# The fourth head of a cross attention: values in halves and other PSUM banks

## The reference

```python
def cross_attend(xn, mk, mv, w_xq, w_xo):
    B, L = xn.shape[:2]
    q = (xn @ w_xq).reshape(B, L, N_X_HEADS, X_HEAD_DIM)
    s = jnp.einsum('bqhd,bkhd->bhqk', q, mk.astype(q.dtype)).astype(F32) * (X_HEAD_DIM ** -0.5)
    p = jax.nn.softmax(s, axis=-1).astype(q.dtype)
    o = jnp.einsum('bhqk,bkhd->bqhd', p, mv.astype(q.dtype))
    return o.reshape(B, L, X_WIDTH) @ w_xo
```

## Time and profile before

| what | us |
|---|---|
| runs, median | 1565.68 |
| profiled execution, whole | 1566.68 |
| profiled execution, its span | 1564.8 |
| TensorE busy in the span | 1517.6 |
| VectorE busy | 653.5 |
| ScalarE busy | 446.4 |
| GpSimd busy | 227.5 |
| mean granted clock of TensorE | 0.988 |

### The profile page before, as it was taken

How to read it: one execution, slowest core, us unless ns; L and a number is a source line. 1 busy time by engine, 2 the same in 40 slices (tenths; PEclk the granted TensorE clock), 3 DMA queues, 4 the chain that set the end, 5 groups by cost and what they waited for, 6 DMA issues and landing times.

```text
span 1564.8 us, 24482 instructions
## 1 busy us (share of the span) xinstructions
PE 1517.6 (97%) x9798; PEld 1446.6 (92%) x9798; DVE 653.5 (42%) x1230; ACT 446.4 (29%) x828; POOL 227.5 (15%) x231
## 2 busy tenths in 40 slices
PE   6999999999899899999999999999999999999997
PEld 6999888888799888878899999999999999999997
DVE  5544666464855433443274322233223432234222
ACT  6422444333421222432143310233102321133122
POOL 2100000133355100034350000000000000000143
PEclk9999999998899999999999999999999999999999
DMA  7554011111231200064531111111111111111102
GB/s 216 180 177 129 28 35 34 41 45 55 87 123 54 94 28 28 14 220 157 175 108 41 53 41 52 43 41 54 41 54 41 40 54 41 54 41 41 54 27 111
DMA packets 153553, 115.49 MB, mean 74 GB/s; under 512 B 13680, under 2 KB 142896, under 8 KB 153200
## 3 DMA queue, kind: packets, MB, share of 16 engines
q1 hardware_dynamic: 142736, 79.11, 17.2%
q0 software_dynamic: 8544, 31.04, 5.8%
q10 hardware_dynamic: 2192, 4.20, 0.8%
HBM read 101.19 MB, written 14.16 MB: 74 GB/s over the span
## 4 chain that ended last, share of the span: by engine, by line
PE 87%; DVE 4%; issue 3%; DMA 2%; ACT 2%; POOL 1%; SPq 0%; DVEq 0%; ACTq 0%; POOLq 0%
PE ps L334 25%; PE ps L335 25%; PE ps L336 25%; PE ps L1165 4%; PE ps L1571 2%; PE ps L1553 1%; DVE wlo L321 1%; PE ps L1253 1%; PE ps L1277 1%; ACT whi L316 1%; DVE rstd L1734 1%; DMA raw<-in_w_xv 1%; DMA raw<-in_w_in 1%; DMA raw<-in_w_xk 1%; PE ps L1632 0%
## 5 line engine op out<-in xcount | busy, mean ns | idle before, releaser
L334 PE MATMUL ps<-xhi,whi 128*128 128x352 f32 x1392 | 457.6, 329 | 5.9 <-DVEq L2250 2.2
L335 PE MATMUL ps<-xlo,whi 128*128 128x352 f32 x1392 | 449.0, 323 | 0.0
L336 PE MATMUL ps<-xhi,wlo 128*128 128x352 f32 x1392 | 448.9, 322 | 0.0
L334 PE MATMUL ps<-yhi,whi 128*128 128x352 f32 x1152 | 377.3, 327 | 5.9 <-DVE wlo L321 2.1
L336 PE MATMUL ps<-yhi,wlo 128*128 128x352 f32 x1152 | 370.3, 321 | 0.0
L335 PE MATMUL ps<-ylo,whi 128*128 128x352 f32 x1152 | 370.1, 321 | 0.0
L334 PEld LDWEIGHTS ps<-xhi,whi 128*128 128x128 f32 x1392 | 263.6, 189 | 15.3 <-issue 11.6
L335 PEld LDWEIGHTS ps<-xlo,whi 128*128 128x128 f32 x1392 | 264.0, 190 | 0.1
L336 PEld LDWEIGHTS ps<-xhi,wlo 128*128 128x128 f32 x1392 | 263.3, 189 | 0.0
L316 ACT ACTIVATE whi<-raw 128x1024 fp32r<-128x1024 f32 x130 | 137.1, 1055 | 387.0 <-PE ps L336 343.6
L334 PEld LDWEIGHTS ps<-yhi,whi 128*128 128x128 f32 x1152 | 216.7, 188 | 10.0 <-DVE wlo L321 3.9
(11 more groups left out here) (260 smaller groups left out, 1295.7 us busy)
## 6 DMA issues: line engine op xcount, KB each, us to landing
raw<-in_w_up SPq DMA_DIRECT2D x32, 512.0 KB
raw<-in_w_down SPq DMA_DIRECT2D x32, 512.0 KB
raw<-in_w_xo SPq DMA_DIRECT2D x16, 512.0 KB
kx<-in_cache_mem_k POOLq DMA_DIRECT2D x16, 512.0 KB, 5.2
raw<-in_w_in SPq DMA_DIRECT2D x14, 512.0 KB
spill<-hT POOLq DMA_DIRECT2D x8, 528.0 KB, 6.3
xin<-in_x_prompt SPq DMA_DIRECT2D x8, 512.0 KB, 7.7
raw<-in_w_xk SPq DMA_DIRECT2D x8, 512.0 KB
```

Source lines behind the costliest of these rows:

```text
L334: pe.matmul(out, whi[:, q, k, :], x1, start=k == 0, stop=False)
L335: pe.matmul(out, whi[:, q, k, :], x2, start=False, stop=False)
L336: mm = pe.matmul(out, wlo[:, q, k, :], x1, start=False, stop=k == KB - 1)
```

## The change

Three things move.

1. `cross_values` can do one half d of its work. Group 5's halves stand ahead of and behind the four score tiles 24 to 27; group 6's halves stand between transpositions. `s_xo` counts up only after the half d=1.
2. Tiles 28 to 31 are transposed into banks 0 and 1 (`turned_bank`), and group 7's values go to banks 4 and 5. The transpositions no longer wait for the copy of the group before.
3. On VectorE `cross_keep(5)` stands behind `cross_max(12)`, on ScalarE behind `cross_exp(12)`, and `cross_pT(7)` ahead of `cross_hi(6, 0)`. The wait for `s_xol` at XRES stands ahead of the transpositions of b=0, kb=1, where it stood ahead of the first `xo_product`.

```diff
         def cross_bank(j, d):
-            return (0 if j == 2 * XH - 1 else 6) + d
+            return (4 if j == 2 * XH - 1 else 6) + d
+
+        def turned_bank(j):
+            return 0 if j == 2 * XH - 1 else 4
...
             for k in range(4):
                 kept_hi(k)
+            cross_exp(12)
             cross_keep(5)
-            cross_exp(12)
             kept_hi(4)
...
             cross_exp(15)
+            cross_pT(7)
             cross_hi(6, 0)
-            cross_pT(7)
...
             def cross_turn(i):
                 pe.wait_ge(s_xp, i + 1)
-                wait(pe, s_xpe, i // 4)
+                if i // 4 < 2 * XH - 1:
+                    wait(pe, s_xpe, i // 4)
...
-            cross_values(5)
+            cross_values(5, (0,))
             pe.wait_ge(s_ev, chunks_before(U_XO))
             i = 3 * NQ
             for t in range(4):
                 cross_scores(i + t)
+            cross_values(5, (1,))
             turns_and_scores(i)
-            cross_values(6)
-            for t in range(4, NQ):
-                cross_turn(i + t)
+            cross_turn(i + 4)
+            cross_turn(i + 5)
+            cross_values(6, (0,))
+            cross_turn(i + 6)
+            cross_turn(i + 7)
+            cross_values(6, (1,))
             cross_values(7)
...
                     pe.wait_ge(s_kl[slot], b // 2 * 16 + 16)
+                    if b == 0 and kb == 1:
+                        pe.wait_ge(s_xol, XRES)
...
             kept_lo(0)
             kept_lo(1)
+            cross_max(12)
             cross_keep(5)
-            cross_max(12)
             kept_lo(2)
             cross_probs(12)
```

More of the change, by code:

```diff
@@ L1004, in cross_pT @@
                 wait(act, s_xo, j - 1)
-                copy(xpT[:, :, cross_half(j)], ps[:, 4:6, :]).then_inc(s_xpe, 1)
+                copy(xpT[:, :, cross_half(j)], ps[:, turned_bank(j):turned_bank(j) + 2, :]).then_inc(s_xpe, 1)
             def cross_keep(j):
@@ L1557, in cross_turn, with cross_values @@
                 pe.wait_ge(s_xp, i + 1)
-                wait(pe, s_xpe, i // 4)
+                if i // 4 < 2 * XH - 1:
+                    wait(pe, s_xpe, i // 4)
                 for a in range(2):
-                    mm = turn(ps[:, 4 + a, (i % 4) * P:(i % 4 + 1) * P], xp[:, i % NQ, a * P:(a + 1) * P])
+                    mm = turn(ps[:, turned_bank(i // 4) + a, (i % 4) * P:(i % 4 + 1) * P], xp[:, i % NQ, a * P:(a + 1) * P])
                 mm.then_inc(s_xpT, 1)
-            def cross_values(j):
+            def cross_values(j, parts=range(2)):
                 pe.wait_ge(s_xpe, j + 1)
@@ L1567, in cross_values @@
                     wait(pe, s_xol, 8 if j == 6 else j)
-                for d in range(2):
+                for d in parts:
                     k = j // 2 * 2 + d
@@ L1571, in cross_values @@
                         mm = pe.matmul(ps[:, cross_bank(j, d), :], mv[:, a, k * P:(k + 1) * P], xpT[:, a, cross_half(j)], start=a == 0, stop=a == 1)
-                mm.then_inc(s_xo, 1)
+                if d == 1:
+                    mm.then_inc(s_xo, 1)
             def turns_and_scores(i):
@@ L1654, in _ @@
                     pe.wait_ge(s_wlo, u + 1)
-                if b == 0:
-                    pe.wait_ge(s_xol, XRES)
                 xo_product(u, c)
```

## The result

The changed kernel took 1568.55 us in the median of 22 runs, the kernel before 1564.86 us in 22 runs beside it. The ratio is 1.0023 (95% interval 1.0016 to 1.0029): slower by 3.6 us (2.5 to 4.5). Measured again later beside other kernels, the ratio was 1.0016 (1.0005 to 1.0028), that is 2.5 us.

A forecast was written before the change was run, and what follows sets the result against it. TensorE is busy nearly throughout; VectorE's in-order queue and GpSimd's chain set its stalls in this stage. Median 1565.68 + 1.58 (VectorE's queue, handed on by GpSimd) + 1.2 (one clock spell) = 1568.5 us, range 1566.3 to 1570.9.

The forecast's parts named there:

- Values(5) in halves: Fourth head of cross attention: scores start 1.71 us earlier, so the first maximum starts just when kept_lo(1) is finished.
- VectorE's hold at cross_keep(5): VectorE waits there for the second half of values(5), so kept_lo(2) and everything queued behind start 1.58 us later.
- ScalarE's inversion costs nothing: ScalarE's cross_keep(5) and kept_hi(4) end before the next exponentials are released at 664.80, so no cost.
- Banks and halves of group 6: The 1.11 us wait for copy 7 goes, but GpSimd's 7.71 us chain still sets the sample keys' start.
- The wait for s_xol before kb=1 costs nothing: Moved wait ahead of kb=1's transpositions: costed at nothing; up to 1 us if GpSimd's cover went.
- One clock spell, 1.2 us: TensorE's clock drops to its lower level after the first new stall, costing 1.2 us, ends 0 and 1.5.
- rival B: Both new stalls drop the clock, the one before the sample keys costing 1.5 us more: 1570.0 us; 27%.
- Nothing gives it back downstream: The sample part starts from TensorE, its loads, splits and copies released by TensorE and VectorE, so all moves along.
- Rival D: The 1.58 us vanish in a later wait that does not move: 1565.7 us; 5%.
- Rival A: No clock spell, only VectorE's queue delay of 1.58 us: 1567.3 us; 20%.
- Rival C: VectorE is not held at cross_keep(5), so the 1.71 us won early reach the stage's end: 1564.0 us; 5%.

The follow-up runs named there:

- p1_halves: Kernel before with only group 5's values in halves and the copy cross_keep(5) moved behind the first maximum (ScalarE likewise); + 2.8 us against the kernel before.
- e1_order: Changed kernel with cross_keep(5) behind the first scaling and second maximum on VectorE, ScalarE reordered to match; - 0.3 us (- 2.2 to 1.4) against the kernel before.
- p2_banks: Kernel before with only the new banks, group 6 in halves and the moved s_xol wait; + 0.5 us (- 1.4 to 2.2) against the kernel before.
- e2_pool: Changed kernel with GpSimd clearing and filling qxm ahead of the wait for kept_lo(5) and the value loads; + 0.9 us (- 0.6 to 2.3) against the kernel before.
- after_again: The changed kernel unaltered, measured once more beside the kernels with constants in its stalls; median 1567.64 us, + 2.5 us against the kernel before.
- fill_first: Changed kernel with matmuls of constants only in the first stall, behind the second half of values(5); + 1.1 us against the kernel before.
- fill_second: Changed kernel with matmuls of constants only in the second stall, before the sample keys (kx); + 1.3 us against the kernel before.
- e13_product_first: Changed kernel with VectorE's, ScalarE's and GpSimd's orders altered and output projection chunk 0 ahead of the keys; 1561.15 us against 1565.96 before, ratio 0.9969.
- filled kernels: Changed kernel with matmuls of constants, read by nothing, in both stalls, measured twice; + 1.4 and + 1.1 us against the kernel before.

## Why the prediction was right

Forecast 1568.5 us, measured 1568.55; slower by 3.6 us by the ratio, where 2.8 were forecast. The prediction's line between same and slower was 0.2%, and the measured 0.23% (0.16 to 0.29) lies across it. Step by step:

- *Values(5) in halves.* Right. 1.71 us earlier scores (1.71 against 3.43 after values(5) start), maximum straight behind kept_lo(1), as worked out.
- *VectorE's hold at cross_keep(5).* Right and shown: 9.43 - 7.95 = 1.48 us at the first transposition where 1.58 was forecast; p1_halves reproduces it, e1_order removes it. Of the 0.1 us, 0.04 is the copy's successor, 0.61 us behind it and not 0.65, and 0.05 the scaling, 1.33 us behind kept_lo(2) where it was 1.38.
- *ScalarE's inversion costs nothing.* Right: the exponentials of pair 13 were released by their maximum at 663.82.
- *Banks and halves of group 6.* Right: the copies' waits go, GpSimd's chain of 7.71 us hides them. It measured 678.76 - 671.03 = 7.73. p2_banks: nothing won, nothing lost at kx. There is a slip in the working, which ends values(7) at 677.5 and then takes the stall from 677.7: its own numbers give 2.2 us and not 2.0. Measured are 2.00.
- *The wait for s_xol before kb=1 costs nothing.* Right in the changed kernel. The prediction's condition, up to 1 us if GpSimd's cover goes, came true in e2_pool with 1.23.
- *One clock spell, 1.2 us.* The size was right: 1.28 (p1_halves) and 1.29 (26.70 - 25.41, after_again) behind the first stall. The place was wrong for the profiled run: behind the second stall, where rival B had 1.5 us and the product shows 28.66 - 27.07 = 1.59. How often, "about as often as not, with a bit more for the 2.5 us one", is neither borne out nor refuted by 3 of 9 open stalls in the profiles (the expectations of fill_first and fill_second, "more than half of the runs", had gone further). By those shares the clock would be worth 2/5 x 1.29 + 1/4 x 1.59 = 0.9 us in the mean, and with the queue 1.44 + 0.9 = 2.3 us. The first measurement, 3.6 (2.5 to 4.5), lies above that, the second, 2.5 (0.8 to 4.4), on it. So the hit of the median within 0.1 us is partly luck: the forecast started from 1565.68 where before was 1564.86 in the 22 runs, 0.8 us too high, and that made up for a change that was 0.9 us larger than forecast (3.7 by the medians). What the rest of about 1.3 us (3.6 - 2.3) in the first measurement is stays open. The Trainium skill (TensorE: Matmul & The Clock Gate, What's actually happening) has the clock low unless activity releases it. The two profiles with both stalls filled agree, with 1.00 from 655 to 690; but the clock stayed at 1.00 behind 6 of the 9 open stalls as well, so they prove little.
- *Nothing gives it back downstream.* Right: nearly all of it is there at the far end (170.64 - 169.31 = 1.33 of 1.44). Rival D's argument overlooks one thing: the wait of 1.39 us near 733 is for wlo, which VectorE makes from a weight unit and not from TensorE's work. It moved along all the same, 1.38 us after the change, and e13_product_first took it away.

Rival A (no spell, + 1.6) is what the filled kernels measure. Rival C fell by the written order, and e1_order shows what it would have brought: 1.12 us at kx.

## What to carry to other kernels

Where a producer is split in two so that something else can start earlier, move the consumer of the *second* half too: an in-order engine that meets it early hands the whole delay to everything behind it. Before a chain is shortened, look at what else the next stage waits for; here GpSimd's clearing and filling of qxm, shown only as "issue", held kx 2.2 us back, and once it was moved another wait took 1.23 us of that. And a wait of 2 us on TensorE is priced with a clock spell behind it, by how often and by how much, not by its length alone.

## What the runs showed of the hardware

The same stall does not always cost the clock. The product at the far end waits 2.20 or 2.21 us in every profile. The granted clock stayed at 1.00 in the profile of before, and fell to the lower level in the changed kernel's:

```profile
820.00:825.00 5.00, 3.53 (x23) 1.00 0.37 105
825.00:830.00 5.00, 4.26 (x17) 0.66 0.02 3
```

Of the 14 profiles here 10 have a spell of 3.4 us at that stall and 4 have none. One execution's profile therefore can't price a change of one or two us by the sum of its span; the distances between fixed places agree within 0.1 us from profile to profile (kx of the changed order, where no spell came before it: 25.41, 25.35, 25.34, 25.39, 25.35).
